# A hybrid trunk kernel: the first x1 turned over a diagonal, its fourth tile and the store of x put elsewhere

## What is computed

```python
def rms_norm(x, g):
    y = xf * lax.rsqrt(jnp.mean(xf * xf, axis=-1, keepdims=True) + NORM_EPS)
    return (y * g)

for i in range(DEPTH):                       # DEPTH = 2
    sh_m, sc_m, gt_m, sh_f, sc_f, gt_f = jnp.split((silu_c @ ada_w[i] + ada_b[i])[:, None, :], 6, axis=-1)
    h = modulate(rms_norm(x, norm_g[i, 0]), sh_m, sc_m)
    y = pool_mixer(...) if kind == KIND_POOL else short_conv_mixer(...)
    x = x + gt_m * rms_norm(y, norm_g[i, 1])             # "x1" in layer 0
    hf = modulate(rms_norm(x, norm_g[i, 2]), sh_f, sc_f) # the MLP's input
    x = x + gt_f * rms_norm(sqrelu_mlp(hf, ffn_w1[i], ffn_w2[i]), norm_g[i, 3])
```

## Time and profile before

| | |
|---|---|
| median of the runs | 938.18 us |
| the profiled execution: its time, its span | 937.01 us, 935.1 us |
| PE busy | 914.9 us (98%) |
| DVE, ACT, POOL busy | 649.3, 431.1, 53.2 us |
| granted TensorE clock | 0.998 of full speed |
| DMA | 170.86 MB, 183 GB/s over the span |

### The profile page before, as it was taken

How to read it: one execution, slowest core, us unless ns; L and a number is a source line. 1 busy time by engine, 2 the same in 40 slices (tenths; PEclk the granted TensorE clock), 3 DMA queues, 4 the chain that set the end, 5 groups by cost and what they waited for, 6 DMA issues and landing times.

```text
span 935.1 us, 11415 instructions
## 1 busy us (share of the span) xinstructions
PE 914.9 (98%) x4623; PEld 753.6 (81%) x4623; DVE 649.3 (69%) x622; ACT 431.1 (46%) x523; POOL 53.2 (6%) x83
## 2 busy tenths in 40 slices
PE   8889999999999999999999999999999999999996
PEld 6658888888888888889888888898888888888885
DVE  6786397589678866696766545757857864783688
ACT  6654484454346333354222224555634624543463
POOL 3002110010001001000101000000000000000001
PEclk9999999999999999999999999999999999999999
DMA  9999889527735576324656531273871661275124
GB/s 306 349 350 359 210 220 327 183 74 215 256 114 139 187 288 226 112 90 158 209 179 217 194 113 46 84 276 123 238 270 34 169 214 57 72 204 174 45 46 179
DMA packets 91403, 170.86 MB, mean 183 GB/s; under 512 B 4270, under 2 KB 34066, under 8 KB 91352
## 3 DMA queue, kind: packets, MB, share of 16 engines
q1 hardware_dynamic: 83912, 155.25, 48.5%
q0 software_dynamic: 7440, 14.89, 8.1%
HBM read 163.81 MB, written 6.32 MB: 182 GB/s over the span
## 4 chain that ended last, share of the span: by engine, by line
PE 52%; DVE 1%; issue 1%; ACT 0%; DVEq 0%
PE ps L674 17%; PE ps L676 17%; PE ps L675 17%; PE ps L768 1%; DVE y L1580 0%; DVE in_lo L1591 0%; PE ps L703 0%; DVE y L1945 0%; DVE xs L1956 0%; ACT in_hi L1209 0%; DVE y L1586 0%; DVE y L1474 0%; DVEq L137 0%; DVE y L1543 0%; DVE st L1949 0%
## 5 line engine op out<-in xcount | busy, mean ns | idle before, releaser
L674 PE MATMUL ps<-in_hi,w_parts 128*128 128x512 f32 (+1 forms) x784 | 290.1, 370 | 0.9 <-DVE in_lo L1591 0.5
L675 PE MATMUL ps<-in_lo,w_parts 128*128 128x512 f32 (+1 forms) x784 | 288.1, 367 | 0.0
L676 PE MATMUL ps<-in_hi,w_parts 128*128 128x512 f32 (+1 forms) x784 | 288.1, 367 | 0.0
L1422 DVE TENSOR_TENSOR w_parts<-raw,w_parts 128x2048 fp32r<-128x2048 f32 x81 | 185.5, 2290 | 125.5 <-ACT w_parts L1102 125.4
L1102 ACT ACTIVATE w_parts<-raw 128x2048 fp32r<-128x2048 f32 x81 | 154.8, 1911 | 214.4 <-PE ps L676 194.4
L674 PEld LDWEIGHTS ps<-in_hi,w_parts 128*128 128x128 f32 x784 | 147.8, 188 | 29.4 <-issue 3.3
L676 PEld LDWEIGHTS ps<-in_hi,w_parts 128*128 128x128 f32 x784 | 147.8, 188 | 24.5
L675 PEld LDWEIGHTS ps<-in_lo,w_parts 128*128 128x128 f32 x784 | 147.8, 189 | 24.1
L674 PE MATMUL ps<-w_parts,ops_hi 128*128 128x512 f32 x280 | 109.1, 389 | 0.2 <-DVE y L1474 0.2
L675 PE MATMUL ps<-w_parts,ops_hi 128*128 128x512 f32 x280 | 109.0, 389 | 0.0
L676 PE MATMUL ps<-w_parts,ops_lo 128*128 128x512 f32 x224 | 87.2, 389 | 0.0
(11 more groups left out here) (203 smaller groups left out, 1040.2 us busy)
## 6 DMA issues: line engine op xcount, KB each, us to landing
raw<-in_ffn_w_dram SPq DMA_DIRECT2D x57, 1024.0 KB, 5.5
ada_raw<-in_ada_w_dram SPq DMA_DIRECT2D x56, 512.0 KB, 6.2
xs<-in_ffn_w_dram SPq DMA_DIRECT2D x14, 1024.0 KB, 5.4
xs<-in_ffn_w_dram POOLq DMA_DIRECT2D x10, 1024.0 KB, 8.7
raw<-in_conv_in_w_dram SPq DMA_DIRECT2D x16, 512.0 KB, 5.3
raw<-in_ada_w_dram SPq DMA_DIRECT2D x4, 1024.0 KB, 11.1
ada_sum<-in_ada_w_dram SPq DMA_DIRECT2D x4, 1024.0 KB, 12.2
win<-in_ada_w_dram SPq DMA_DIRECT2D x4, 1024.0 KB, 11.9
```

What stands on the lines that cost most here:

```text
L674: nc.tensor.matmul(o, hi, b_hi, start=start, stop=False, skip_group_check=on)
L675: nc.tensor.matmul(o, hi, b_lo, start=False, stop=False, skip_group_check=on)
L676: return nc.tensor.matmul(o, lo, b_hi, start=False, stop=stop, skip_group_check=on)
L1422: nc.vector.tensor_tensor(w_lo[:, u % W_SLOTS, :], raw_of(u), w_hi[:, u % W_SLOTS, :].bitcast(F32), ALU.subtract).then_inc(w_lo_ready, 1)
```

## The change

DVE makes x1 of the fourth tile directly behind the first two reciprocals, ahead of `columns(8)` and the first input, and ACT takes that tile's root ahead of `first_hi(0)`. Instead of a normed tile, DVE now writes a diagonal matrix, the identity times the reciprocals (`first_diag`), into the first 128 columns of the tile in `y_tok`; PE then makes the turned and normed block as a matmul of x1 itself (`xs`, stationary) with that diagonal (moving) in place of a transpose of the normed tile. The store of x waits for the last of the eight turns, since PE now reads `xs`, and is issued behind the load of unit 4.

```diff
             def save_x(layer):
                 if layer == 0:
-                    sp.wait_ge(x1_norm, NT)
+                    sp.wait_ge(x1_turned, len(FIRST_TURNED))
                     sp.wait_ge(x1_sq, NT)
...
             for u in range(4, UNITS):
-                for layer in (0, 1):
-                    if u == FFN_U[layer] + 3:
-                        save_x(layer)
+                if u == FFN_U[1] + 3:
+                    save_x(1)
                 if not seven_of(u):
                     load(u)
+                    if u == FFN_U[0] + 3:
+                        save_x(0)
...
             def turn_first(side, pair):
-                pe.wait_ge(x1_norm, 2 * side + 2)
+                pe.wait_ge(x1_diag, 2 * side + 2)
...
-                        tr = nc.tensor.transpose(o[:, n, toks(t)], y_tok[:, 2 * side + t, (2 * pair + n) * P:(2 * pair + n + 1) * P], ident[:, :])
+                        tr = nc.tensor.matmul(o[:, n, toks(t)], xs[:, 2 * side + t, (2 * pair + n) * P:(2 * pair + n + 1) * P], y_tok[:, 2 * side + t, 0:P], start=True, stop=True)
...
             first_root(2)
+            first_root(3)
             first_hi(0)
             copy_first(0, 2)
-            first_root(3)
...
-            def first_norm(t):
+            def first_diag(t):
                 dve.wait_ge(x1_rms, t + 1)
                 nc.vector.reciprocal(st0[:, 7, t:t + 1], st0[:, 6, t:t + 1]).then_inc(x1_rcp, 1)
                 dve.wait_ge(x1_rcp, t + 1)
-                nc.vector.tensor_scalar(y_tok[:, t, :], xs[:, t, :], st0[:, 7, t:t + 1], None, ALU.mult).then_inc(x1_norm, 1)
+                nc.vector.tensor_scalar(y_tok[:, t, 0:P], ident[:, :], st0[:, 7, t:t + 1], None, ALU.mult).then_inc(x1_diag, 1)
...
-            first_norm(0)
-            first_norm(1)
+            first_diag(0)
+            first_diag(1)
+            first_x(3)
             columns(8)
             first_input(0)
+            first_diag(2)
             first_lo(0)
-            first_x(3)
-            first_norm(2)
-            first_norm(3)
+            first_diag(3)
             first_input(1)
```

More of the change, by code:

```diff
@@ L248, in trunk @@
         y0_sq, y0_copied, y0_gated, y0_sum, y0_rms, y0_rcp = sem("y0_sq"), sem("y0_copied"), sem("y0_gated"), sem("y0_sum"), sem("y0_rms"), sem("y0_rcp")
-        x1_new, x1_sq, x1_rms, x1_rcp, x1_norm = sem("x1_new"), sem("x1_sq"), sem("x1_rms"), sem("x1_rcp"), sem("x1_norm")
+        x1_new, x1_sq, x1_rms, x1_rcp, x1_diag = sem("x1_new"), sem("x1_sq"), sem("x1_rms"), sem("x1_rcp"), sem("x1_diag")
         x1_turned, xt_copied, f_made, f_hi, f_lo = sem("x1_turned"), sem("xt_copied"), sem("f_made"), sem("f_hi"), sem("f_lo")
```

## The result

The changed kernel takes 942.74 us, the median of 5 runs (941.68 to 944.6). Its ratio to the kernel before is 1.0043, with an interval of 1.0028 to 1.0058: slower by 2.6 to 5.4 us. The time lies inside the range of 939.3 to 943.5. It is 1.3 us beyond the forecast of 941.4 (+3.2) by the medians and 0.8 by the ratio, which gives +4.0. In a second measurement on another occasion the same kernel gave 942.93 and a ratio of 1.0040 (1.0024 to 1.0056). The profiled execution took 942.74 with a span of 940.6, 5.5 over that of the kernel before.

A forecast was written before the change was run, and what follows sets the result against it. The prediction took a chain of PE work to bound the stage: 4.0 us of added records less 0.76 of waits gives +3.2, from a median of 938.18 to 941.4 us. The range was 939.3 to 943.5.

The forecast's parts named there:

- forecast of 941.4 (+3.2): Whole kernel: median of 938.18 us plus 3.2; the forecast as a case, +2.0 to +4.6, had chance 0.75.
- What bounds the stage: First turn to first 512-column matmul: a chain of PE work, PE busy 20.12 of 20.14 us.
- The price of 4.0 us: PE's turns, 62.8 to 82.9 us: 32 more records at 0.124 us each, +4.0 us of PE work.
- Neither bound: Price of PE's turns: 2.8 us if idle times of 0.41 absorbed 1.2; 5.4 if each turn ended with another 0.17.
- The gain of 0.76: PE's waits in the stage: 0.55 us from an earlier first turn, 0.09 at `add_up(15)`, 0.12 at `part(1, 0)`.
- The fourth x1 and the store: DVE's earlier `first_x(3)` costs nothing, covered by 0.3 us; SP's later store costs 0, with 2 us to spare.
- The bound on the store: Behind SP's store: if all shifts by 8.9 us, POOL's additions for N end at 128.0, before ACT's copy at 130.0.
- One record each: PE's turns: matmuls over a diagonal run at the transpose's pace, leaving only the 0.76 gain: 937.4 us; chance 0.06.
- PE waiting after all: PE's stage: waits on landings take up half of the 3.2: +1.6, 939.8 us; chance 0.10.
- Four times a transpose: PE's turns: a plain fp32 matmul costs four transposes, 11.9 in place of 4.0: +11.1, 949.3 us; chance 0.04.
- The sum: Whole kernel: 4.0 us of added PE work less 0.76 of waits gives +3.2 us.
- a new idle time behind 100 us: PE after 100 us: a new idle time there would prove the forecast wrong; no size given.

The follow-up runs named there:

- doubled transposes: Kernel before with each of the 32 transposes issued twice into the same place: 942.02 us, ratio 1.0037.
- the tiny records: Kernel before with 16 tiny plain fp32 matmuls (32 records) between the last two add_ups ahead of stay_busy, where PE sat idle: 939.25 us, ratio 1.0012.
- the halved doubling: Kernel before with only 16 of the 32 transposes issued twice: 939.81 us, ratio 1.0015.
- the order: Kernel before with the fourth tile's x1 and root moved ahead of the first input, norms and transposes as they were: 938.83 us, ratio 1.0003.
- the store: Kernel before with only the store of x moved behind unit 4's load and waiting for the last of the eight turns: 937.94 us, ratio 1.0001.
- both: Kernel before with the fourth x1 and root moved ahead and the store of x moved later, without the diagonal: 939.1 us, ratio 1.0004.
- 22 stay_busy: Kernel before with 22 in place of 6 plain fp32 matmuls in the stay_busy ahead of turn_up(8), 32 records more: 943.55 us, ratio 1.0043.
- 16 records fewer: Changed kernel without the stay_busy of six ahead of turn_up(8), and with an early one of three cut to one: 943.68 us, ratio 1.0048 to the kernel before.
- turns and store: Changed kernel with DVE's and ACT's old order, keeping the turns over a diagonal and the later store: 942.46 us, ratio 1.0037 to the kernel before.
- the transpose of x1: Changed kernel with each turn a transpose of x1 against the identity, diagonals made but unused, scaling left out: 939.03 us, ratio 0.9998 to the kernel before.
- the filler: Kernel before with seven more plain fp32 stay_busy matmuls in PE's idle time of 1.95 us: 938.42 us, ratio 0.9995.

## Why the prediction was right

- **What bounds the stage.** As read: pure PE work. Doubled transposes (2.8 without the first turn) and the diagonal (3.2) cost what their records last, less the small waits.
- **The price of 4.0 us.** From the first turn's next step to the last `add_up` 3.17 more, with the two small waits of 0.21 used up in it, and 0.52 in the first turn: 3.9 for 32 second records. The `stay_busy` row x12 was the right one to go by. Neither bound came: no 0.41 was used up (2.8), and the 0.17 behind a turn went instead of coming eight times (5.4).
- **The gain of 0.76.** The first turn came 0.53 closer to `turn_up(8)` (0.55 forecast); the other waits went. The diagonal took 0.29, as its nearest row had it.
- **The fourth x1 and the store.** Nothing that can be told, as forecast. What it costs to move the fourth x1 without the diagonals stays open (0 to about 1 us). The bound on the store, all behind it 8.9 us later, was far too wide: N's additions came only 1.2 later, the late start of the profile left out.
- **The rivals.** One record each and PE waiting after all fell with the x64 row and with the doubled transposes. Four times a transpose, the figure that the Trainium skill has on its page TensorE: Matmul & The Clock Gate, section Terms, fell too: the stage gives about two. What the Trainium skill advises in Perfetto Trace Analysis, section Transposes, holds here: +3.9 us for 32 of them.
- **What was missed.** The sum took everything behind 83 us as a plain shift. The term that it lacked is the 0.95 us near 160 us. By the table above, 32 more instructions in PE's program had moved an instruction packet onto a load that PE waits for. The prediction had named a new idle time behind 100 us as a sign against it, and this was one, against the completeness of the sum. With it, 3.16 + 0.95 = 4.1, against 4.0 by the ratio and 4.6 by the medians. Without it the forecast of +3.2 met the stage's 3.16, and the whole time only within the range.

## What to carry to other kernels

Before an operation is swapped for one that does more at once, look for the new form in the old trace and count its records: a plain fp32 matmul of 128 by 128 was two where a transpose was one, and in a stage of pure PE work 1.9 us less on DVE gave 0.53 us back to PE, for 3.9 us more of PE's own work. Reckon a gain only from the waits of the engine that bounds the stage; here they held 0.76 us. And when a few tenths of a per cent remain, compare single waits far behind the change too: here they grew with 32 more instructions on PE, wherever these stood ahead of them.

## What the runs showed of the hardware

- With a packet of the instruction queue beside it, a 1 MB load of POOL's queue landed about 1 us later: 10.2 to 10.7 us to ACT's split in six profiles, 9.2 to 9.7 in the eight without. That the packet is the cause rests on that table, on the tiny records and on the halved doubling; no run moved the packet alone.
- The granted clock fell to 0.5 from about 59 us on, for 3 to 7 us, in 8 of 14 profiles (with the order, the store, both, the doubled transposes, 22 stay_busy, the changed kernel's second one, the tiny records, and 16 records fewer), behind an idle time of PE of 1.95 us (0.98 with the tiny records) that a load's landing ended, and after other short ones. It did not in the profile before, the changed kernel's first one, turns and store, the transpose of x1, the halved doubling, though these five had the same idle time, nor with the filler. `stay_busy` took up to 2.6 us for its 12 records in such a profile instead of 1.4. The clock also fell at earlier places, as from 24 to 36 us with the transpose of x1.
- Added transposes into the same place cost 0.10 us a record, second records of plain fp32 matmuls 0.113 (0.107 and 0.121 with the waits that they used up).
